# A mixture-of-experts block in fp32: expert blocks of 32 slots on four column groups instead of 64 on two, with the down product moved into the next block's gate-up

## The chip, the core and the metric

The kernel runs on one core of a Trainium2 chip. TensorE (PE) multiplies, VectorE (DVE) and ScalarE (ACT) work on elements, GpSimd (POOL) makes constants and some loads, and SyncE (SP) issues nearly all loads of weights. The metric is device time of one execution in microseconds. The kernel before takes 1511.01 us, the median of 3 runs from 1509.67 to 1511.81.

## The reference

One layer of a model of width 1024 on 256 tokens: a modulated norm, sparse attention and gated linear attention side by side, their merge, and a mixture of 32 experts, in fp32. The change touches the experts alone:

```python
logits = (xt @ router_w + router_b)            # xt 256 x 1024, 32 experts
top_v, top_e = lax.top_k(logits, TOP_K)        # TOP_K = 4
wts = jax.nn.softmax(top_v, axis=-1)
...                                            # tokens sorted by expert, padded to blocks
def expert_block(args):
    xb, e = args
    hgu = xb @ w_gate_up[e] + b_gate_up[e]     # w_gate_up[e] 1024 x 2048
    gate, up = jnp.split(hgu, 2, axis=-1)
    gate = jnp.minimum(gate, 7.0)
    up = jnp.clip(up, -7.0, 7.0)
    act = (up + 1.0) * (gate * jax.nn.sigmoid(1.702 * gate))
    return act @ w_down[e] + b_down[e]         # w_down[e] 1024 x 1024
out = segment_sum(ys * pw, ptok)               # weighted sum over each token's 4 experts
x = x + gt2 * out
```

The 256 x 4 assignments spread unevenly over the experts. All 32 experts get tokens, so all their weights, 32 x 12 MiB, are read once.

## The kernel before, in words

Everything up to the router (about 460 us) is written out in order and isn't touched. Its tables are made on VectorE: `table_n` holds the number of blocks, `table_e` the expert of each block, `table_w` what the load semaphores must have reached for that expert, `table_used` the block from which an expert's slots may be overwritten. A block is 64 slots (`SLOTS`) of one expert; an expert has as many blocks as its tokens need. Each engine then runs a loop over blocks, with the counts in registers.

One block on PE is: `gate_up` (L1380), eight pieces of 128 rows of the weights, each against 64 gathered tokens (`xg`); the 64 columns stand twice side by side on the array, so two column groups (q = 0, 1) work on different halves of the output. Between the first piece and the second stand the bias (L1387) and the scatter of the block before (L1355). Then come the gather of the next block's tokens (L1339, a product of `h2` with the 0/1 matrix `sel`), transposes of the slot weights (L1395), of the gathered tokens (L1348) and of the hidden values (L1402), and the down product (L1409), four pieces of 256 rows. ScalarE copies between the steps (`gx`, `xg`, `actT`, `selwT`, `ysb`) and computes the sigmoid; VectorE limits and multiplies the hidden values (`gcl`, `ucl`, `act_t`), makes `sel` and `selw` for the next block and, in `add_rows`, multiplies the scattered rows by `gt2` and adds them into `xs`.

The weights have one set of slots: eight `gu_slot` of 1 MiB (2048 columns, so runs of 8 KB) and four `dn_slot` of 1 MiB (two rows of 1024 for each partition, runs of 4 KB). SyncE goes through experts 1 to 31 in order and, for each slot, waits until its last load has landed and until the last block of the expert before has used it (`gu_used`, `dn_used`), then issues the load. It waits in order: a slot that isn't free holds all behind it.

Of the kernel before, what the change touches and what calls it, by code (L numbers as in the profile page):

```python
# [24 lines left out]
SLOTS = 64  # L25
# [42 lines left out]
def hybrid_block(nc, x, c, w_ada, b_ada, norm1_g, w_in, w_gate_lr, b_gate, gla_norm_g, w_branch_a, w_branch_b, w_out,  # L68
# [10 lines left out]
    MAXB = E + T * TOP_K // SLOTS  # L79
    NP2 = 4  # L80
# [16 lines left out]
    with ExitStack() as ctx:  # L97
# [11 lines left out]
        gu_slot = [sb(f"gu_slot{j}", 8 * j, [P, 2048]) for j in range(8)]  # L109
# [66 lines left out]
        def small(name, shape, dt=F32):  # L176
# [42 lines left out]
        le = sb("le", 187.5, [MAXB + 1, E])  # L219
        eofc = sb("eofc", 187.75, [MAXB + 1, 1])  # L220
        eofw = sb("eofw", 177, [MAXB + 1, 3 * E])
# [3 lines left out]
        eof = small("eof", [1, MAXB + 1])  # L225
        need_w = small("need_w", [1, MAXB + 1])
        table_e = small("table_e", [1, MAXB + 1], I32)
        table_w = small("table_w", [1, MAXB + 1], I32)
# [4 lines left out]
        of_block = small("of_block", [3 * E, MAXB + 1])  # L233
# [6 lines left out]
        xg = sb("xg", 128, [P, 4, P])  # L240
        gx = sb("gx", 130, [P, 512])
        gcl = sb("gcl", 132, [P, 512])
        sig = sb("sig", 134, [P, 512])
        ucl = sb("ucl", 136, [P, 512])
        act_t = sb("act_t", 138, [P, 512])
        actT = sb("actT", 140, [P, 4, P])
        ysb = sb("ysb", 142, [P, 512])
        sel = sb("sel", 144, [P, TT, SLOTS])
        selw = sb("selw", 144.5, [P, TT, 2, SLOTS])
# [4 lines left out]
        junk2 = sb("junk2", 132, [P, D])  # L254
# [3 lines left out]
        sum_bank = [[bank[6], bank[7]], [bank[4], bank[5]]]  # L258
# [23 lines left out]
        gu_in = [sem(f"gu_in{j}") for j in range(8)]  # L282
        dn_in = [sem(f"dn_in{j}") for j in range(4)]
        bgu_in, bd_in = sem("bgu_in"), sem("bd_in")
        gu_used = [sem(f"gu_used{j}") for j in range(8)]
        dn_used = [sem(f"dn_used{j}") for j in range(3)]
        bias3_ready = sem("bias3_ready")
        row_scaled, row_added = [sem(f"row_scaled{q}") for q in range(2)], sem("row_added")
# [5 lines left out]
        actT_full, actT_out, y_full, y_out, sc_full, acc_out = (  # L294
            sem(n) for n in ("actT_full", "actT_out", "y_full", "y_out", "sc_full", "acc_out"))
# [5 lines left out]
        def tile(name):  # L301
            return bank[NUMBER[name] % 8]
# [28 lines left out]
        def _(sp):  # L331
            def load_expert_piece(e, j):

                if j < 8:
                    sp.dma_start(gu_slot[j][:], w_gate_up[0, e, j * P:(j + 1) * P, :] if isinstance(e, int) else  # L335
                                 w_gate_up[0, ds(e, 1), j * P:(j + 1) * P, :].rearrange("a p n -> p (a n)")).then_inc(gu_in[j], 16)
                else:
                    i = j - 8
                    rows = slice(2 * i * P, 2 * (i + 1) * P)
                    sp.dma_start(dn_slot[i][:], w_down[0, e, rows, :].rearrange("(i p) n -> p i n", p=P) if isinstance(e, int) else  # L340
                                 w_down[0, ds(e, 1), rows, :].rearrange("a (i p) n -> p (a i) n", p=P)).then_inc(dn_in[i], 16)

            for n, (kind, i, last) in enumerate(PIECES):
                if n >= NP2:
                    wait_tile(sp, PIECES[n - NP2][2])
                sp.dma_start(piece[n % NP2][:], piece_source(kind, i)).then_inc(piece_in[n % NP2], 16)
                if kind in ("wa", "wb"):
                    wait_tile(sp, "o3")
                    load_expert_piece(0, 8 + 2 * (kind == "wb") + i)
            for j in range(8):  # L350
                user = [last for n, (_, _, last) in enumerate(PIECES) if n % NP2 == j // 2][-1]
                wait_tile(sp, user)
                load_expert_piece(0, j)
# [15 lines left out]
        def _(pool):  # L369
# [34 lines left out]
            for i in range(3):  # L404
# [6 lines left out]
                                allow_small_or_imprecise_dtypes=True))  # L411
            for i in range(3):
# [7 lines left out]
        def _(act):  # L420
# [200 lines left out]
            act.wait_ge(gath_full, 1)  # L621
            step(A(gx[:], bank[2][:], ACT.Copy), gx_out)
            act.wait_ge(gxT_full, 1)
            step(A(xg[:].rearrange("p j s -> p (j s)"), bank[3][:], ACT.Copy), xg_out)
            act.wait_ge(tables_ready, 1)
            nb = act.value_load(table_n[0:1, 0:1], min_val=1, max_val=MAXB)
            with act.Fori(0, nb) as g:
                g1_ = act.snap(g + 1)
                g2_ = act.snap(g + 2)
                act.wait_ge(gcl_ready, g1_)  # L630
                A(sig[:], gcl[:], ACT.Sigmoid, scale=ALPHA).then_inc(sig_ready, 1)  # L631
                act.wait_ge(gath_full, g2_)
                A(gx[:], bank[2][:], ACT.Copy).then_inc(gx_out, 1)  # L633
                act.wait_ge(gxT_full, g2_)
                A(xg[:].rearrange("p j s -> p (j s)"), bank[3][:], ACT.Copy).then_inc(xg_out, 1)  # L635
                act.wait_ge(actT_full, g1_)
                A(actT[:].rearrange("p c s -> p (c s)"), bank[4][:], ACT.Copy).then_inc(actT_out, 1)  # L637
                act.wait_ge(selwT_full, g1_)
# [817 lines left out]
```

## Time and profile before

| | |
|---|---|
| median of 3 runs | 1511.01 us |
| span of the profiled execution | 1508.0 us |
| last matmul of the expert stage ends | 1496.8 us |
| expert stage starts (first gather) | 463.2 us |
| PE, weight loads, DVE, ACT busy | 92%, 41%, 30%, 17% of the span |
| mean granted clock of PE | 0.987 |
| DMA moved | 483.37 MB, mean 321 GB/s |
| of it expert weights | 384 loads of 1 MiB |

The profile holds one execution, of which the span is given; no time of its own beside the span is on the page, and the median of the runs is 3.0 us above that span. Shares are means over stages with different limits, so the rows further down are taken stage by stage. An fp32 product of PE shows as two instructions, which is why counts of matmul instructions are twice those in the code.

### The profile page before, as it was taken

To read this page: it belongs to the slowest core of one execution; us is meant where nothing else is said; L and a number is where in the kernel's file an instruction comes from. 1 tells how busy PE (TensorE), PEld (TensorE's weight loads), DVE (VectorE), ACT (ScalarE), POOL (GpSimd) and SP (SyncE) were. 2 spreads that over 40 slices of the span, in tenths; PEclk is the share of its full clock that TensorE was granted. 3 is DMA by queue.
4 is the path that set the end of the run, shared out by engine and by line. 5 is a ranking of instruction groups with operands and counts; after the bars stand their busy time and mean duration, and the time that the engine had idled before them with its cause. 6 is when DMAs were issued, how large, how long until landed. Compare 5 with 4: busy or idle time off the path is not lost.

```text
span 1508.0 us, 17239 instructions
## 1 busy us (share of the span) xinstructions
PE 1394.2 (92%) x6390; PEld 618.8 (41%) x6391; DVE 449.9 (30%) x965; ACT 253.3 (17%) x433; POOL 10.6 (1%) x34
## 2 busy tenths in 40 slices
PE   0999999999987999999999999999999999989996
PEld 0788545777742333333333333333333333323331
DVE  0160024112234333233233333332332332323233
ACT  1330014210011111111111111111111111111111
POOL 0000000000000000000000000000000000000000
PEclk9999999999987999999999999999999999999998
DMA  8734343587743584999699999979999999999995
GB/s 273 279 112 168 118 161 112 173 281 287 295 187 128 207 334 159 418 416 419 277 399 418 418 416 419 419 312 417 416 419 418 417 416 419 419 417 416 419 419 206
DMA packets 117687, 483.37 MB, mean 321 GB/s; under 512 B 14738, under 2 KB 14866, under 8 KB 84802
## 3 DMA queue, kind: packets, MB, share of 16 engines
q1 hardware_dynamic: 108368, 477.13, 79.4%
q0 software_dynamic: 1056, 4.06, 0.9%
q10 hardware_dynamic: 8242, 1.89, 0.6%
q8 instruction: 15, 0.25, 0.1%
q14 instruction: 6, 0.05, 0.0%
HBM read 482.00 MB, written 1.05 MB: 320 GB/s over the span
## 4 chain that ended last, share of the span: by engine, by line
PE 72%; DMA 10%; SPq 8%; ACT 4%; ACTq 2%; issue 1%; DVE 1%; DVEq 0%
PE bank L1380 23%; PE bank L1073 14%; PE bank L1409 13%; DMA gu_slot<-in_w_gate_up 10%; PE bank L1082 7%; SPq L335 4%; SPq L340 4%; PE bank L1339 4%; PE bank L1355 3%; PE bank L1061 2%; PE bank L1348 1%; ACT gx L633 1%; ACT xg L635 1%; ACT actT L637 1%; ACTq L428 1%
## 5 line engine op out<-in xcount | busy, mean ns | idle before, releaser
L1380 PE MATMUL bank<-gu_slot,xg 128*64 128x512 f32 x2304 | 518.2, 597 | 16.3 <-DMA gu_slot<-in_w_gate_up 15.4
L1380 PEld LDWEIGHTS bank<-gu_slot,xg 128*64 128x64 f32 x2304 | 159.2, 137 | 363.7 <-issue 310.5
L1409 PE MATMUL bank<-dn_slot,actT 128*64 128x512 f32 x1152 | 255.1, 595 | 24.7 <-ACT actT L637 24.7
L993 DVE TENSOR_TENSOR rowt<-bank,gt 128x512 f32<-128x512 f32 x144 | 92.7, 685 | 398.6 <-PE bank L1355 397.3
L1073 PE MATMUL bank<-hT,piece 128*128 128x256 f32 x704 | 153.7, 380 | 0.0
L1409 PEld LDWEIGHTS bank<-dn_slot,actT 128*64 128x64 f32 x1152 | 79.5, 137 | 177.2 <-issue 143.9
L1073 PEld LDWEIGHTS bank<-hT,piece 128*128 128x128 f32 x704 | 133.3, 190 | 19.9 <-issue 2.0
L631 ACT ACTIVATE sig<-gcl 128x512 f32<-128x512 f32 x36 | 22.7, 630 | 569.3 <-DVE gcl L1011 569.3
L1011 DVE TENSOR_SCALAR gcl<-bank 128x512 f32<-128x512 f32 x36 | 24.9, 691 | 272.1 <-PE bank L1380 272.1
L997 DVE TENSOR_TENSOR xs<-xs,rowt 128x512 f32<-128x512 f32 x144 | 93.1, 688 | 2.5
L1082 PE MATMUL bank<-piece,hT 128*128 128x512 f32 x192 | 83.4, 593 | 0.0
L1339 PE MATMUL bank<-h,sel 128*64 128x512 f32 x296 | 71.6, 605 | 3.0 <-DVE sel L965 3.0
L1355 PE MATMUL bank<-ysb,selwT 64*128 64x512 f32 x288 | 72.1, 619 | 0.0
L641 ACT ACTIVATE ysb<-bank 128x512 f32<-128x512 f32 x36 | 21.5, 597 | 248.9 <-PE bank L1409 248.9
L1061 PE MATMUL bank<-piece,silc 128*32 128x512 f32 x192 | 24.8, 642 | 34.1 <-DVE silc L674 34.1
L1082 PEld LDWEIGHTS bank<-piece,hT 128*128 128x128 f32 x192 | 36.2, 190 | 44.3 <-issue 44.2
L631 ACT ACT_TABLE_LOAD x36 | 46.2, 1283 | 0.9 <-issue 0.3
L1339 PEld LDWEIGHTS bank<-h,sel 128*64 128x64 f32 x296 | 21.5, 139 | 45.7 <-issue 45.7
L1355 PEld LDWEIGHTS bank<-ysb,selwT 64*128 64x128 f32 x288 | 25.0, 188 | 32.5 <-issue 32.5
L1348 PE MATMUL bank<-ident,gx 128*128 128x128 f32 x148 | 24.7, 290 | 12.5 <-ACT gx L633 11.8
L1073 PE MATMUL bank<-yaT,piece 128*128 128x256 f32 x128 | 28.0, 379 | 0.0
L1073 PE MATMUL bank<-ybT,piece 128*128 128x256 f32 x128 | 28.0, 379 | 0.0
(274 smaller groups left out, 771.6 us busy)
## 6 DMA issues: line engine op xcount, KB each, us to landing
gu_slot<-in_w_gate_up SPq DMA_DIRECT2D x256, 1024.0 KB, 17.2
dn_slot<-in_w_down SPq DMA_DIRECT2D x128, 1024.0 KB, 17.1
piece<-in_w_in SPq DMA_DIRECT2D x17, 2048.0 KB, 7.8
piece<-in_w_ada SPq DMA_DIRECT2D x12, 2048.0 KB, 15.0
piece<-in_w_branch_a SPq DMA_DIRECT2D x2, 2048.0 KB, 7.9
piece<-in_w_branch_b SPq DMA_DIRECT2D x2, 2048.0 KB, 8.6
piece<-in_w_out SPq DMA_DIRECT2D x2, 2048.0 KB, 10.3
xs<-in_x ACTq DMA_DIRECT2D x1, 1024.0 KB, 13.2
```

Of the source, the lines that this page charges most:

```text
L335: sp.dma_start(gu_slot[j][:], w_gate_up[0, e, j * P:(j + 1) * P, :] if isinstance(e, int) else w_gate_up[0, ds(e, 1), j * P:(j + 1) * P, : ...
L340: sp.dma_start(dn_slot[i][:], w_down[0, e, rows, :].rearrange("(i p) n -> p i n", p=P) if isinstance(e, int) else w_down[0, ds(e, 1), rows ...
L631: A(sig[:], gcl[:], ACT.Sigmoid, scale=ALPHA).then_inc(sig_ready, 1)
L993: ins = V.tensor_tensor(rowt[:, t, :], sum_bank[t][q][:], gt2[:, cols_], ALU.mult)
L997: ins = V.tensor_tensor(xs[:, t, cols_], xs[:, t, cols_], rowt[:, t, :], ALU.add)
L1061: ins = M(ps[32 * q:32 * q + 32, :], silc[:, k, :], w[:, k, :], start=(r == 0), stop=(r == 1), tile_position=(0, 32 * q))
L1073: ins = M(ps[:, f * T:(f + 1) * T], w[:, k, a:a + P], src[:, k, :], start=(k == 0), stop=(k == KT - 1))
L1082: ins = M(ps[:], src[:, k, t * P:(t + 1) * P], w[:, k, :], start=(k == 0), stop=(k == KT - 1))
L1339: ins = M(bank[2][64 * q:64 * q + 64, :], sel[:, t, :], h2[:, t, 512 * q:512 * q + 512], start=(t == 0), stop=(t == TT - 1))
L1355: ins = M(sum_bank[t][q][:], selwT[64 * q:64 * q + 64, t * P:(t + 1) * P], ysb[64 * q:64 * q + 64, :], start=True, stop=True)
L1380: ins = M(bank[u][64 * q:64 * q + 64, :], xg[:, k % 4, 64 * (k // 4):64 * (k // 4) + 64], gu_slot[k][:, cols_], start=(k == 0), stop=(k == ...
L1409: ins = M(bank[5][64 * q:64 * q + 64, :], actT[:, f % 4, 64 * (f // 4):64 * (f // 4) + 64], dn_slot[f // 2][:, f % 2, 512 * q:512 * q + 51 ...
```

## The change

Blocks have 32 slots (`SLOTS = 32`, `GROUPS = 4`). The 32 columns of a block stand on four column groups, each for a quarter of the outputs. Gate-up takes its weights in four pieces of 256 rows; a partition holds two neighbouring rows, so a `gu_slot` is 2 MiB in runs of 16 KB, and a `dn_slot` 1 MiB in runs of 8 KB. The transposes pick every second column to match (`(i r) -> r i`).

The loop is skewed: the down product of a block is done within the gate-up of the next, after its second piece and the next gather; its scatter follows the last gate-up piece. Block 0 is written out ahead of the loop, and the last down and scatter behind it. The four sum banks stay in PSUM through the whole loop: `bias_rows` starts them, each scatter adds (`start=False`), and VectorE reads them once at the end, so `add_rows` is gone. The copy of `actT` moves from ScalarE to VectorE. Elementwise steps have 256 columns instead of 512.

```diff
-SLOTS = 64
+SLOTS = 32
+GROUPS = 4
...
-        gu_slot = [sb(f"gu_slot{j}", 8 * j, [P, 2048]) for j in range(8)]
+        gu_slot = [sb(f"gu_slot{j}", 16 * j, [P, 2, 2, D]) for j in range(4)]
...
+        hid_bank, y_bank, turn_bank, xgT_bank = bank[4], bank[5], bank[6], bank[7]
+        sum_bank = [[bank[0], bank[1]], [bank[2], bank[3]]]
...
+            def load_gate_up(e, q):
+                rows = slice(2 * P * q, 2 * P * (q + 1))
+                sp.dma_start(gu_slot[q][:].rearrange("p r u n -> p (r u n)"),
+                             w_gate_up[0, e, rows, :].rearrange("(p r) n -> p (r n)", r=2) if isinstance(e, int) else
+                             w_gate_up[0, ds(e, 1), rows, :].rearrange("a (p r) n -> p (a r n)", r=2)).then_inc(gu_in[q], 16)
...
             with sp.Fori(1, E) as e:
                 free = sp.value_load(table_used[0:1, ds(e, 1)], min_val=1, max_val=MAXB + 1)
-                for j in range(12):
-                    here, used = (gu_in[j], gu_used[j]) if j < 8 else (dn_in[j - 8], (dn_used + [y_full])[j - 8])
-                    sp.wait_ge(here, 16 * e)
-                    sp.wait_ge(used, free)
-                    load_expert_piece(e, j)
+                for q in range(4):
+                    sp.wait_ge(gu_in[q], 16 * e)
+                    sp.wait_ge(gu_used[q] if q < 3 else gu_full, free)
+                    load_gate_up(e, q)
+                for q in range(4):
+                    sp.wait_ge(dn_in[q], 16 * e)
+                    sp.wait_ge(dn_used[q] if q < 3 else y_full, free)
+                    load_down(e, q)
...
+            def hidden(full_count, count):
+                dve.wait_ge(gu_full, full_count)
+                V.tensor_scalar(gcl[:], hid_bank[:, 0:256], LIMIT, None, ALU.min).then_inc(gcl_ready, 1)
+                V.tensor_scalar(ucl[:], hid_bank[:, 256:512], LIMIT, -LIMIT, ALU.min, ALU.max).then_inc(ucl_ready, 1)
+                dve.wait_ge(sig_ready, count)
+                V.tensor_tensor(gcl[:], gcl[:], sig[:], ALU.mult).then_inc(gs_ready, 1)
+                dve.wait_ge(gs_ready, count)
+                V.scalar_tensor_tensor(act_t[:], ucl[:], 1.0, gcl[:], ALU.add, ALU.mult).then_inc(act_ready, 1)
+                dve.wait_ge(actT_full, count)
+                V.tensor_copy(actT[:].rearrange("p r s -> p (r s)"), turn_bank[:, 0:256]).then_inc(actT_out, 1)
...
+            def gate_up(q, landed):
+                pe.wait_ge(gu_in[q], landed)
+                for r in range(2):
+                    for c in range(GROUPS):
+                        ins = M(hid_bank[32 * c:32 * c + 32, :], xg[:, r, 32 * q:32 * q + 32],
+                                gu_slot[q][:, r, :, 256 * c:256 * c + 256], start=(q == 0 and r == 0), stop=(q == 3 and r == 1))
+                ins.then_inc(gu_used[q] if q < 3 else gu_full, 1)
...
+            def down(landed):
+                for pair in range(2):
+                    for h in range(2):
+                        pe.wait_ge(dn_in[2 * pair + h], landed)
+                    for r in range(2):
+                        for half in range(2):
+                            for h in range(2):
+                                c = 2 * pair + h
+                                a = 32 * (2 * half + h)
+                                ins = M(y_bank[a:a + 32, :], actT[:, r, 32 * c:32 * c + 32],
+                                        dn_slot[c][:, r, 512 * half:512 * half + 512],
+                                        start=(pair == 0 and r == 0), stop=(pair == 1 and r == 1))
+                                if r == 1 and half == 1:
+                                    ins.then_inc(dn_used[c] if c < 3 else y_full, 1)
...
+            with pe.Fori(1, nb) as g:
...
+                pe.wait_ge(xg_out, g1_)
+                gate_up(0, landed)
+                gate_up(1, landed)
+                pe.wait_ge(actT_out, g)
+                pe.wait_ge(sel_ready, g2_)
+                gather()
+                pe.wait_ge(selw_out, g)
+                down(landed_before)
+                gate_up(2, landed)
                 pe.wait_ge(selw_ready, g1_)
+                gate_up_bias()
+                gate_up(3, landed)
+                pe.wait_ge(y_out, g)
+                scatter()
                 pe.wait_ge(gx_out, g2_)
                 gather_transposes()
+                weight_transposes()
                 pe.wait_ge(act_ready, g1_)
+                hidden_transposes()
```

How the instructions stand now and before, on PE, within one turn of the block loop (names: `gu_slot`, `dn_slot` weights, `xg` gathered tokens, `h_85` or `h_81` the tokens `h2`, `bias_66` or `bias_62` the biases; a row is one or more equal instructions, with the semaphores it waits for). Before:

```order
L1380 MATMUL bank<-gu_slot_60,xg 64x512 [waits gu_in7]
L1380 MATMUL bank<-gu_slot_60,xg 64x512 x3
L1391 REGISTER_ALU
L1339 MATMUL bank<-h_85,sel 64x512 [waits sel_ready]
L1339 MATMUL bank<-h_85,sel 64x512 x3
L1395 MATMUL bank<-ident,selw 128x128 [waits ucl_ready]
L1348 MATMUL bank<-ident,gx 128x128 [waits gx_out]
L1348 MATMUL bank<-ident,gx 128x128 x3
L1402 MATMUL bank<-ident,act_t 128x128 [waits act_ready,acc_out]
L1402 MATMUL bank<-ident,act_t 128x128 x3
L1409 MATMUL bank<-dn_slot_61,actT 64x512 [waits dn_in0,actT_out]
```

Now, from the top of the turn to behind the down product's start:

```order
L1398 MATMUL bank<-gu_slot_53,xg 32x512 [waits gu_in0,xg_out]
L1398 MATMUL bank<-gu_slot_53,xg 32x512 x7
L1398 MATMUL bank<-gu_slot_54,xg 32x512 [waits gu_in1]
L1398 MATMUL bank<-gu_slot_54,xg 32x512 x7
L1472 REGISTER_ALU [waits actT_out]
L1371 MATMUL bank<-h_81,sel 32x256 [waits sel_ready]
L1371 MATMUL bank<-h_81,sel 32x256 x7
L1417 MATMUL bank<-dn_slot_57,actT 32x512 [waits dn_in1,dn_in0,selw_out]
```

The gather and the down product have moved between the second and the third gate-up piece, and the down product there is that of the block before.

On SyncE, one expert's loads before:

```order
L335 ISA [waits gu_used6,gu_in6]
L335 DMA gu_slot_59<-in_w_gate_up 128x2048
L335 ISA [waits gu_used7,gu_in7]
L335 DMA gu_slot_60<-in_w_gate_up 128x2048
L340 ISA [waits dn_used0,dn_in0]
L340 DMA dn_slot_61<-in_w_down 128x2x1024
```

and now:

```order
L338 ISA [waits gu_used2,gu_in2]
L338 DMA gu_slot_55<-in_w_gate_up 128x4096
L338 ISA [waits gu_full,gu_in3]
L338 DMA gu_slot_56<-in_w_gate_up 128x4096
L344 ISA [waits dn_used0,dn_in0]
L344 DMA dn_slot_57<-in_w_down 128x2048
```

The order of the loads is the same; they are eight for an expert instead of twelve, and each waits for one piece of twice the rows in gate-up.

## Rows read from the trace of the kernel before

**Rows 1.** The page: busy us and share of PE, and GB/s in 40 slices

```profile
PE 1394.2 (92%) x6390; PEld 618.8 (41%) x6391; DVE 449.9 (30%) x965; ACT 253.3 (17%) x433; POOL 10.6 (1%) x34
GB/s 273 279 112 168 118 161 112 173 281 287 295 187 128 207 334 159 418 416 419 277 399 418 418 416 419 419 312 417 416 419 418 417 416 419 419 417 416 419 419 206
```

**Rows 2.** Chain that ended last, one block: start us, us, what

```profile
499.91 1.72 PE bank L1380 x8
501.63 0.44 PE bank L1387 x4
502.06 1.92 PE bank L1355 x8
503.98 12.17 PE bank L1380 x56
516.15 1.74 PE bank L1339 x8
...
518.56 0.67 PE bank L1348 x4
...
527.55 1.72 PE bank L1380 x8
```

**Rows 3.** The same chain late in the span, two experts apart

```profile
1391.90 25.29 DMA gu_slot<-in_w_gate_up
...
1452.17 25.26 DMA gu_slot<-in_w_gate_up
```

**Rows 4.** Windows: stretch us, busy us (instructions) by engine, granted clock, DMA share, GB/s

```profile
509.50:530.00 20.50, 19.48 (x96) 6.94 (x94) 3.96 (x10) 4.53 (x7) 0.00 (x0) 1.00 0.00 0
563.50:585.50 22.00, 20.98 (x104) 7.45 (x102) 5.02 (x12) 4.53 (x7) 0.00 (x0) 1.00 0.00 2
...
1040.00:1480.00 440.00, 410.29 (x1910) 136.99 (x1906) 137.33 (x271) 68.03 (x105) 0.00 (x0) 1.00 1.02 418
```

**Rows 5.** Timeline of SyncE's queue, gate-up loads of experts 1 and 2

```profile
473.28 16.63 SPq L335 DMA_DIRECT2D gu_slot<-in_w_gate_up  x8
...
529.51 15.67 SPq L335 DMA_DIRECT2D gu_slot<-in_w_gate_up  x8
```

**Rows 6.** Timeline of PE, four column groups in use at L1061

```profile
41.51 1.93 PE L1061 MATMUL bank<-piece,silc 128*32 128x512 f32 x16
43.37 2.84 PE L1099 MATMUL bank<-inv,modp 128*128 128x1 f32 x24
```

**Rows 7.** Timeline, one elementwise step of 512 columns

```profile
1419.21 0.69 DVE L1011 TENSOR_SCALAR gcl<-bank 128x512 f32<-128x512 f32 x1 [9.40 <-PE bank L1380]
```

**Rows 8.** Windows: gate-up pieces (first two), down pieces (last)

```profile
443.00:450.00 7.00, 4.16 (x24) 2.10 (x24) 2.98 (x7) 2.85 (x7) 0.00 (x0) 0.59 1.01 428
1400.00:1415.00 15.00, 13.90 (x65) 4.20 (x64) 5.16 (x8) 1.88 (x2) 0.00 (x0) 1.00 1.01 422
1418.00:1426.00 8.00, 6.98 (x36) 2.67 (x34) 3.96 (x10) 2.65 (x5) 0.00 (x0) 1.00 1.02 409
```

**Rows 9.** DMA issues in 462 to 478: KB, us to landing

```profile
gu_slot<-in_w_gate_up SPq DMA_DIRECT2D x1, 1024.0 KB, 4.8
```

**Rows 10.** Windows around the router and the first block

```profile
440.00:444.00 4.00, 0.15 (x2) 0.00 (x0) 2.55 (x10) 2.73 (x6) 0.00 (x0) 1.00 0.88 328
...
462.00:469.30 7.30, 4.79 (x12) 1.57 (x12) 2.69 (x23) 1.20 (x2) 0.00 (x0) 0.50 0.00 0
469.30:475.00 5.70, 5.66 (x16) 1.82 (x18) 0.00 (x0) 1.28 (x1) 0.00 (x0) 0.50 0.18 26
475.00:480.00 5.00, 5.00 (x26) 1.62 (x24) 3.54 (x6) 0.00 (x0) 0.00 (x0) 1.00 0.54 197
```

**Rows 11.** Chain ahead of the first block (its start at 469.34)

```profile
463.17 3.70 PE bank L1339 x8
...
469.34 3.68 PE bank L1380 x8
```

**Rows 12.** Chain at the end, VectorE's second half

```profile
1496.86 1.30 DVE rowt L1024 x2
```

More of the change, by code:

```diff
@@ L239, in hybrid_block @@
         rowt = sb("rowt", 176, [P, TT, 512])
[L240 to L247, printed above, removed]
+        gx = sb("gx", 128, [P, 256])
+        xg = sb("xg", 129, [P, 2, P])
+        gcl = sb("gcl", 130, [P, 256])
+        ucl = sb("ucl", 131, [P, 256])
+        sig = sb("sig", 132, [P, 256])
+        act_t = sb("act_t", 133, [P, 256])
+        actT = sb("actT", 134, [P, 2, P])
+        ysb = sb("ysb", 136, [P, 512])
         sel = sb("sel", 144, [P, TT, SLOTS])
-        selw = sb("selw", 144.5, [P, TT, 2, SLOTS])
+        selw = sb("selw", 144.5, [P, TT, GROUPS, SLOTS])
         selwT = sb("selwT", 145.5, [P, T])
@@ L1324, in _ @@
             pe.wait_ge(eofc_ready, 1)
[L1325 removed]
+            full(M(ps[0:3 * E, 0:NT], eofw[:], ident[0:NT, 0:NT], start=True, stop=True))
             ps = begin("wt")
@@ L1332, in _, with gather @@
             full(ins)
[L1335 removed]
+            def gather():
                 for t in range(TT):
[L1338 to L1339 removed]
+                    for c in range(GROUPS):
+                        ins = M(turn_bank[32 * c:32 * c + 32, 0:256], sel[:, t, :], h2[:, t, 256 * c:256 * c + 256],
                                 start=(t == 0), stop=(t == TT - 1))
[L1341 to L1342 removed]
@@ L1353, in scatter @@
+            def scatter(last=False):
                 for t in range(TT):
@@ L1366, in _ @@
             gather_transposes()
-            with pe.Fori(0, nb) as g:
+            pe.wait_ge(xg_out, 1)
+            pe.wait_ge(selw_ready, 1)
+            for q in range(3):
+                gate_up(q, landed0)
+            gate_up_bias()
+            gate_up(3, landed0)
+            pe.wait_ge(sel_ready, 2)
+            gather()
+            pe.wait_ge(bd_in, 16)
+            wait_out(pe, "wt")
+            bias_rows()
+            pe.wait_ge(gx_out, 2)
+            gather_transposes()
+            weight_transposes()
+            pe.wait_ge(act_ready, 1)
+            hidden_transposes()
+            with pe.Fori(1, nb) as g:
                 g1_ = pe.snap(g + 1)
@@ L1403, in _ @@
-                ins.then_inc(actT_full, 1)
-                pe.wait_ge(actT_out, g1_)
-                for f in range(KT):
-                    if f % 2 == 0:
-                        pe.wait_ge(dn_in[f // 2], landed)
-                    for q in range(2):
-                        ins = M(bank[5][64 * q:64 * q + 64, :], actT[:, f % 4, 64 * (f // 4):64 * (f // 4) + 64],
-                                dn_slot[f // 2][:, f % 2, 512 * q:512 * q + 512], start=(f == 0), stop=(f == KT - 1))
-                    if f % 2 == 1:
-                        ins.then_inc(dn_used[f // 2] if f < KT - 1 else y_full, 1)
@@ L1428, in _ @@
-            bias_rows(0)
-            pe.wait_ge(selw_out, pe.snap(nb + 1))
-            pe.wait_ge(y_out, pe.snap(nb + 1))
-            last_rows(0)
-            bias_rows(1)
-            last_rows(1)
+                hidden_transposes()
+            pe.wait_ge(actT_out, nb)
+            pe.wait_ge(selw_out, nb)
+            landed_last = pe.value_load(table_w[0:1, ds(nb - 1, 1)], min_val=16, max_val=16 * E)
+            down(landed_last)
+            pe.wait_ge(y_out, nb)
+            scatter(last=True)
```

253 lines of the change are left out of this document (119 added, 134 removed).

## The prediction, written before the result was known

> **What bounds the kernel now.** I read the page first. TensorE (PE) is busy 92% of the span and the DMA rate sits near 418 GB/s from the middle of the span on [rows 1], so two limits lie close together. The chain of waits through one expert block tells which one binds early: a block of 64 slots takes 27.63 us (499.91 to 527.55), all of it PE work but for a few copies [rows 2]. Each expert's weights are 12 MiB, 12.58 MB, and late in the span two experts lie 60.27 us apart in that chain (1391.90 to 1452.17), 30.13 us each [rows 3]. So single-block experts settle on the DMA rate, and PE waits for it little. The stretches show the other half: the DMA moved nothing in 509.5 to 530 and in 563.5 to 585.5, but 418 GB/s in 1040 to 1480 [rows 4]. SyncE's queue says why: it starts expert 1's gate-up loads at 473.28 and can start expert 2's only at 529.51, two blocks of 27.63 us and 1 us later [rows 5]. There is one set of weight slots. While an expert has a further block, its slots are in use and the next expert's load can't start.
>
> How many blocks each expert has is set by the input. The reference's router on its own input gives the 32 experts 2, 127, 71, 46, 36, 3, 24, 88, 50, 22, 16, 23, 33, 11, 17, 99, 61, 5, 28, 28, 7, 3, 9, 30, 27, 16, 15, 37, 2, 20, 16, 52 tokens. In blocks of 64 that is 36, with two blocks for experts 1, 2, 7 and 15. In blocks of 32 it is 49: four blocks for experts 1 and 15, three for 2 and 7, two for 3, 4, 8, 12, 16, 27 and 31, one for the rest.
>
> **A block after the change.** Gate-up stays at 64 matmul instructions of 512 columns, on four column groups. With two groups 56 took 12.17 us, 217 ns each [rows 2]. The trace has four groups in use at L1061: 16 in 1.86 us from start to start, 116 ns each with the drain of so short a run [rows 6]; I take half of 217, 109 ns: 7.0 us. Down is 32 of the same: 3.5. Bias: half of 0.44, 0.2. Gather: 16 instructions of 256 columns, a quarter of 1.74/8 each, 0.9. Scatter stays 1.9. Transposes: 6 for 10 at 0.67/4, 1.0. Sum 14.5 us. The loop turn now stands behind the last transposes, with two register loads ahead of the first gate-up and no long matmul run to hide them; unseen on PE, between 0 and 0.8 us, I take 0.5. Block: **15.0 us** (14.5 to 16). The activation chain costs nothing while it is covered: gcl, sig, product and act_t at 256 columns are some 0.4 us each (0.69 at 512 [rows 7]), 2.1 us in all, beside scatter and four transposes, 2.6 us; uncovered it would add up to 2 us. The four multiplies and four adds of expert rows into xs on VectorE go away (the sums stay in PSUM); they lay beside PE, whose wait for them has no row in the block's chain. PE's total falls from 36 x 27.6 = 995 us to 49 x 15.0 = 735, so PE is no longer the bound: the weights of experts 1 to 31, 390 MB, need 933 us at 418 GB/s. What decides is how fast they come and how often the queue stands still.
>
> **The transfers.** 8 KB packets came at 422 GB/s and 4 KB ones at 409 [rows 8]; 8.39/0.422 + 4.19/0.409 = 30.1 us, the cycle of [rows 3]. Over 16 engines that is 311 ns for 8 KB and 160 for 4 KB, so about 10 ns of each packet is not bytes. 16 KB would take 612 ns, 428 GB/s, and a cycle 19.6 + 9.9 = **29.5 us**. No trace here has 16 KB packets. The bounds are 30.1 (longer runs give nothing) and 28.9 (no cost beside the bytes: 151 ns per 4 KB, 434 GB/s); I take the value the packet cost gives.
>
> **When the queue stands still.** Let L be when the last gate-up piece of an expert lands; its down pieces follow by L + 9.9. PE finishes that piece by L + 2.3, scatter, transposes and loop turn take 3.4, the next block's first gate-up piece 1.75: L + 7.5, and SyncE can issue at L + 7.9. A lone 1 MB load landed 4.8 us after its issue [rows 9]; 2 MB takes 2.5 more, 7.3. Unbroken the next piece would land at L + 14.8. An expert of two blocks thus loses 0.4 us, of three 0.4 + 15.0 = 15.4, of four 30.4. Experts 1 to 30: 6 x 0.4 + 2 x 15.4 + 2 x 30.4 = **94 us** of idle queue. Before it was 20.5 and 22 us behind experts 1 and 2 [rows 4], and the dips to 277 and 312 GB/s in [rows 1] are experts 7 and 15. The smaller blocks make the largest experts hold the slots longer while the stream needs them free.
>
> **The clock.** After 4 us with hardly a matmul (440 to 444) the granted clock is at half, 1.2 GHz; it is still there in 462 to 469.3, where PE works with gaps, and in 469.3 to 475, and back at full behind that, when PE has worked unbroken [rows 10]. In the new kernel PE is idle from about L + 6 to L + 14.8 in each single-block expert, so I expect its first gate-up piece at 1.2 GHz. The second piece lands at L - 9.9; behind it come the gather and the first half of down, which must free the first down slot by L - 2.35 (its next load would land at L + 2.45, 4.8 us after the issue). At full clock that is 1.75 + 0.9 + 1.75 + 0.4 us, L - 5.1, in time. At half clock all through it is 3.5 + 1.8 + 3.5 + 0.4, L - 0.7, 1.7 us late. From the second piece on PE works without a gap until past L, and in such a stretch the clock came back, so I take a value near the warm end, 0.35 us for each of the 26 experts among 1 to 30 with one or two blocks: **9 us** (0 to 44).
>
> The Trainium skill bears on this (TensorE: Matmul & The Clock Gate, Loop structure matters more than you think): a DMA wait ahead of each tile's matmuls makes every tile run cold. By that rule alone the term would be its upper end, 44 us; [rows 10] agree that a gap brings the half clock, and disagree that unbroken work stays cold.
>
> **Start and end.** Before the first block, at the half clock: gather 3.70 to 2.0 us, two copies and the transposes from there to 469.34 2.5 to 1.5 [rows 11], against 0.8 for two more register loads ahead of the first selection and the eight memsets that now stand first (an estimate, no row prices them there). So the block starts at 467.5 instead of 469.34. Its first gate-up piece (3.7 us, twice as many instructions as the eight of L1380 in [rows 11] at half the time each) is free at 471.2 instead of 473.28 [rows 5]; its 2 MB lands at 478.5, so the stream counts from 473.6. A late first down slot of expert 1 costs 1. End of the stream: 473.6 + 31 x 29.5 + 94 + 1 + 9 = 1492.1. Expert 31 has a second block, and its down is deferred: down 3.5, gate-up and bias 3.7, turn 3.0, actT 0.7, down 3.5, ysb 1.0, half the scatter 1.0, VectorE's first half twice 1.3, and from the start of its second half to the end 1508.0 - 1496.86 = 11.1 as now [rows 12]. That is 30.0: span 1522. The profiled execution has a span of 1508.0 and the median is 1511.0; with the same 3.0 us around it the time is **1525 us**, 14 more than before.
>
> **Rivals.** *Faster transfers.* With no cost beside the bytes a cycle is 28.9, 19 us less in all, and 1506. It needs the packet cost to be per packet and nothing else at 422 GB/s; that 8 KB packets gave 428 while PE was busy 4.16 us of 7 [rows 8] speaks for it, that they gave only 422 beside a busy PE against it. It decides the sign at a cycle of 28.95 us, or at 29.25 if the clock term is nil too. This is the case on the other side, 0.24 with its neighbours. The Trainium skill (DMA: Bandwidth & Descriptors, Where 436 GB/s comes from) gives 435 GB/s as the ceiling of the ports; an estimate from it is the same 28.9 us per expert. No row here shows more than 428 over a few us.
>
> *Cold clock.* If the clock stays at half until past L, every single-block cycle is 1.7 us longer and the time 1560: 0.12. For it: PE works only half of each cycle. Against it: nine us without a gap lie ahead of L.
>
> *Four groups give less than twice two.* At 20 us a block, each block that the queue waits out costs 5 us more (6 of them), and the way to the first release 1.2 us at ten experts: with the end some 45 us, 1570: 0.05. L1061 speaks against it.
>
> *Even.* Cycle 29.3 and no clock term, 1508 to 1514: 0.12.
>
> *The change does less than it says.* If 16 KB packets are no better (30.1), 31 x 0.6 adds 19: 1544, inside the forecast's side, 0.12.
>
> The forecast itself holds 0.35, between 1514 and 1538. A measurement of this kernel can't tell less than about 0.2%, 3 us, from no change. Faster (under 1508) 0.24, same 0.12, slower 0.64. The range for 8 in 10 runs from 1502, the fast transfers, to 1553, past the 16 KB case and short of the cold one.
>
> **What would show it.** In the changed profile: PE busy near 75% of the span and about half of a single-block stretch, DMA near full in most slices; four stretches without transfers, about 30, 15, 15 and 30 us long, behind experts 1, 2, 7 and 15; 29.5 us from one single-block expert to the next; some 16 gate-up instructions in 1.75 us; the granted clock falling to half once in each cycle; gate-up waiting for the DMA most. I am wrong if the cycle is under 29 us, if the clock holds the cycle over 31, or if the stretches without transfers sum to under 75 us.

## The result, and the profile after

The changed kernel takes **1539.4 us** (median of 4 runs, 1536.5 to 1548.5) against 1510.4 us for the kernel before on the same chip: ratio **1.0198** (95% interval 1.0180 to 1.0217), slower. The forecast was 1525 us (1502 to 1553), slower with 0.64. Sign and mechanism were right, the size was half of what came. The profiled execution has a span of 1534.7 us; the forecast span was 1522.

The page after (busy us and share by engine; GB/s in 40 slices; gate-up's matmuls with the idle time before them and its releaser; their DMA issues with KB and us to landing):

```profile
PE 1194.2 (78%) x8222; PEld 563.1 (37%) x8223; DVE 281.0 (18%) x852; ACT 191.7 (12%) x427; POOL 10.7 (1%) x35
GB/s 268 274 110 165 156 118 110 179 298 327 233 164 282 61 315 333 404 427 411 245 405 427 426 414 422 350 144 406 421 421 426 418 413 421 425 421 410 426 425 94
L1398 PE MATMUL bank<-gu_slot,xg 128*32 128x512 f32 x3136 | 428.3, 674 | 274.4 <-DMA gu_slot<-in_w_gate_up 241.7
gu_slot<-in_w_gate_up SPq DMA_DIRECT2D x128, 2048.0 KB, 15.8
```

PE fell from 92% of the span [rows 1] to 78%, though 49 blocks are computed instead of 36; gate-up now waits for transfers for 242 us. PE no longer bounds the whole: the dips in the GB/s row (61; 315 with 333; 245; 350 with 144) are the places where nothing comes.

Four stretches, a single-block stretch and a two-block expert, in windows (stretch, its length, busy us and instructions on PE, PEld, DVE, ACT, POOL, granted clock, DMA share, GB/s):

```profile
503.30:533.70 30.40, 28.03 (x256) 11.44 (x252) 6.51 (x22) 4.11 (x10) 0.00 (x0) 1.00 0.00 1
565.60:581.60 16.00, 14.84 (x138) 6.03 (x134) 3.25 (x11) 2.06 (x5) 0.00 (x0) 1.00 0.00 2
735.20:750.00 14.80, 13.64 (x129) 5.61 (x125) 3.25 (x11) 2.05 (x5) 0.00 (x0) 1.00 0.01 3
990.80:1021.80 31.00, 28.59 (x264) 11.71 (x260) 6.50 (x22) 4.11 (x10) 0.00 (x0) 1.00 0.00 1
1080.00:1340.00 260.00, 150.31 (x1102) 45.00 (x1105) 27.65 (x95) 17.27 (x43) 0.00 (x0) 0.76 1.00 421
612.00:643.00 31.00, 28.65 (x264) 11.72 (x260) 6.50 (x22) 4.11 (x10) 0.00 (x0) 1.00 0.97 403
```

The stretches without transfers behind experts 1, 2, 7 and 15 are 30.4, 16.0, 14.8 and 31.0 us: 92 us, where about 30, 15, 15 and 30 stood in the forecast. They answer to the 20.5 and 22 us of [rows 4]. These windows hold only the time in which nothing comes; their edges, where little comes, are not in the 92 us. In the single-block stretch PE works 58% of the time and the DMA all of it.

The chain of waits through one block inside a multi-block expert (start us, us, what), to be read beside [rows 2]:

```profile
547.64 3.64 PE bank L1398 x32
551.28 0.86 PE bank L1371 x16
552.14 3.43 PE bank L1417 x32
555.57 1.72 PE bank L1398 x16
557.29 0.22 PE bank L1404 x4
557.51 1.72 PE bank L1398 x16
559.23 1.92 PE bank L1427 x8
561.14 0.43 PE bank L1378 x2
561.58 0.22 PE bank L1384 x2
561.80 0.24 PE bank L1389 x2
562.04 1.20 issue
563.24 3.64 PE bank L1398 x32
```

Gate-up 7.1, gather 0.9, down 3.4, scatter 1.9, transposes 0.9, bias 0.2: 14.4 us of work. Behind it PE does nothing for 1.20 us that the profile can name: the loop turn with its register loads. The block is **15.60 us**.

When SyncE issues the first gate-up load of an expert (us), before and after, with two kernels that come below. An expert's interval, below, is the time to the first load of the next expert. Right behind an expert of several blocks it comes out short (23.9 us for expert 9), since SyncE then issues into an empty queue; so only sums over stretches that begin and end behind such experts can be compared to a few tenths:

| first load of expert | before | after | loop turned | before, long runs |
|---|---|---|---|---|
| 1 | 473.28 | 471.63 | 474.56 | 474.89 |
| 3 | 584.78 | 580.97 | 577.79 | 585.78 |
| 9 | 778.22 | 780.78 | 769.60 | 779.86 |
| 13 | 888.75 | 900.25 | 888.99 | 890.75 |
| 16 | 1001.12 | 1021.25 | 1008.13 | 1002.22 |
| 28 | 1350.78 | 1382.45 | 1363.47 | 1341.17 |
| 31 | 1440.25 | 1464.43 | 1445.85 | 1429.73 |
| end of span | 1508.0 | 1534.7 | 1515.3 | 1499.7 |

Rows of after of the kind from which that table and the intervals below come, experts 1, 4 and 5 (SyncE's queue; start us, us of issuing):

```profile
471.63 5.67 SPq L338 DMA_DIRECT2D gu_slot<-in_w_gate_up  x4
...
612.18 9.98 SPq L338 DMA_DIRECT2D gu_slot<-in_w_gate_up  x4
...
643.34 9.97 SPq L338 DMA_DIRECT2D gu_slot<-in_w_gate_up  x4
```

Up to expert 9 the rows of the two stay within 4 us of each other (the changed kernel 1.7 and 3.8 us ahead, then 2.6 behind). From 9 to 13 the kernel before goes at its PE's 27.6 us an expert, with weights that came in while an expert had two blocks; the changed one takes 29.9 us on average, near the transfers' time, and loses 9 us. From 13 to 16, over expert 15 with four blocks, it loses 8.6 more. The rest of the span adds 6.6.

### The profile page after: what moved, and what is told of

It is laid out like the page before. It is cut to its first block, busy times and chain, and to the rows that moved or that the text cites. A ratio compares the mean times of both kernels' runs of the same rounds, so it can differ in the third digit from the quotient of the medians.

```text
span 1534.7 us, 20943 instructions
## 1 busy us (share of the span) xinstructions
PE 1194.2 (78%) x8222; PEld 563.1 (37%) x8223; DVE 281.0 (18%) x852; ACT 191.7 (12%) x427; POOL 10.7 (1%) x35
## 3 DMA queue, kind: packets, MB, share of 16 engines
q10 hardware_dynamic: 8242, 1.89, 0.6%
## 4 chain that ended last, share of the span: by engine, by line
PE 63%; DMA 26%; issue 4%; SPq 3%; ACTq 2%; DVE 1%; ACT 1%; DVEq 0%
DMA gu_slot<-in_w_gate_up 26%; PE bank L1398 17%; PE bank L1105 14%; PE bank L1417 11%; PE bank L1114 7%; PE bank L1427 4%; PE bank L1371 3%; PE bank L1093 2%; SPq L344 1%; ACTq L438 1%; PE bank L1378 1%; SPq L338 1%; SPq L361 1%; PE bank L1306 1%; PE bank L1295 1%
## 5 line engine op out<-in xcount | busy, mean ns | idle before, releaser
L1398 PE MATMUL bank<-gu_slot,xg 128*32 128x512 f32 x3136 | 428.3, 674 | 274.4 <-DMA gu_slot<-in_w_gate_up 241.7
L1398 PEld LDWEIGHTS bank<-gu_slot,xg 128*32 128x32 f32 x3136 | 111.4, 118 | 519.2 <-issue 432.4
L1417 PE MATMUL bank<-dn_slot,actT 128*32 128x512 f32 x1568 | 177.8, 592 | 1.4 <-DVE actT L1017 1.4
L1010 DVE TENSOR_SCALAR gcl<-bank 128x256 f32<-128x256 f32 x49 | 20.8, 425 | 815.5 <-PE bank L1398 815.5
L1427 PE MATMUL bank<-ysb,selwT 64*128 64x512 f32 x392 | 97.4, 615 | 0.7 <-ACT ysb L649 0.7
L1417 PEld LDWEIGHTS bank<-dn_slot,actT 128*32 128x32 f32 x1568 | 55.8, 110 | 92.9 <-issue 86.1
L1371 PE MATMUL bank<-h,sel 128*32 128x256 f32 x800 | 57.4, 404 | 4.4 <-DVE sel L991 4.4
L1371 PEld LDWEIGHTS bank<-h,sel 128*32 128x32 f32 x800 | 31.1, 122 | 51.4 <-issue 45.5
L649 ACT ACTIVATE ysb<-bank 128x512 f32<-128x512 f32 x49 | 29.3, 597 | 152.5 <-PE bank L1417 152.5
L1017 DVE COPY actT<-bank 128x256 f32<-128x256 f32 x49 | 20.8, 425 | 49.7 <-PE bank L1389 49.7
L998 DVE TENSOR_SCALAR selw<-iota,slot_id,wts 128x128 f32<-128x128 f32 x100 | 29.6, 337 | 0.0
## 6 DMA issues: line engine op xcount, KB each, us to landing
xs<-in_x ACTq DMA_DIRECT2D x1, 1024.0 KB, 13.1
```

The costliest lines, as they stand in the source:

```text
L649: A(ysb[:], y_bank[:], ACT.Copy).then_inc(y_out, 1)
L998: ins = V.tensor_scalar(selw[:, t, :, :], iota[:].unsqueeze(1).to_broadcast([P, GROUPS, SLOTS]), slot_id[:, t, ds(e, 1)], wts[:, t, ds(e, ...
L1010: V.tensor_scalar(gcl[:], hid_bank[:, 0:256], LIMIT, None, ALU.min).then_inc(gcl_ready, 1)
L1017: V.tensor_copy(actT[:].rearrange("p r s -> p (r s)"), turn_bank[:, 0:256]).then_inc(actT_out, 1)
L1371: ins = M(turn_bank[32 * c:32 * c + 32, 0:256], sel[:, t, :], h2[:, t, 256 * c:256 * c + 256], start=(t == 0), stop=(t == TT - 1))
L1398: ins = M(hid_bank[32 * c:32 * c + 32, :], xg[:, r, 32 * q:32 * q + 32], gu_slot[q][:, r, :, 256 * c:256 * c + 256], start=(q == 0 and r = ...
```

## Experiments

**The changed kernel with short runs.** Loads and transposes as before the change, everything else as after.

```diff
-                sp.dma_start(gu_slot[q][:].rearrange("p r u n -> p (r u n)"),
-                             w_gate_up[0, e, rows, :].rearrange("(p r) n -> p (r n)", r=2) if isinstance(e, int) else
+                sp.dma_start(gu_slot[q][:].rearrange("p r u n -> p r (u n)"),
+                             w_gate_up[0, e, rows, :].rearrange("(r p) n -> p r n", r=2) if isinstance(e, int) else
...
-                    ins = nc.tensor.transpose(xgT_bank[:, r * P:(r + 1) * P], gx[:].rearrange("p (i r) -> p r i", r=2)[:, r, :],
+                    ins = nc.tensor.transpose(xgT_bank[:, r * P:(r + 1) * P], gx[:, r * P:(r + 1) * P],
```

> The changed kernel with runs of 8 KB (gate-up) and 4 KB (down) again, in the same eight loads for an expert. Theory (about 10 ns of each packet is not bytes): a single-block expert takes 0.6 us more, 30.4 us, at 21 of the 31 experts; those bound by PE's blocks don't change: +13 us, 1552. Rival (long runs or 2 MB pieces hurt the transfers, and that is why the time came out above the forecast): faster than the changed kernel, 1520 to 1536.

Measured 1560.8 us (1558.1 to 1564.6), ratio to the kernel before 1.0330 (1.0307 to 1.0354): 21 us slower than with long runs. In the single-block stretch (the same columns as above):

```profile
1080.00:1340.00 260.00, 154.77 (x1162) 46.47 (x1154) 29.26 (x99) 18.50 (x45) 0.00 (x0) 0.76 1.01 412
```

412 GB/s instead of 421. So the long runs pay, and by more than the 13 us expected from the packet cost; how much of it is packets is measured below.

**Both kernels with one block for each expert.** Tokens beyond the first block of an expert are left out, so 32 blocks in each.

```diff
             chain(V.tensor_reduce(blocks[:], over[:], AX.X, ALU.add))
+            chain(V.tensor_scalar(blocks[:], blocks[:], 1.0, None, ALU.min))
```

> The changed kernel with at most one block for each expert: 32 blocks instead of 49, tokens beyond the 32nd of an expert are left out. Theory (the loss is the queue standing still for experts of several blocks): no stretch without transfers, 30 cycles of 29.9 us from the first last-piece landing at 493 us, and 26 us behind the last: 1417 us, and the granted clock low in every cycle. Rival (clock or transfers themselves): cycles above 30.5 us, over 1435.

> The kernel before with at most one block for each expert: 32 blocks instead of 36, tokens beyond the 64th left out. Theory: transfers bind at 30.13 us an expert from the start, 934 us of stream from 476 and 17 to 20 us behind it: 1430 us, so that without further blocks the changed kernel is the faster by 10 to 15 us. Rival (the changed kernel is slower in itself): 1415 or less here.

Measured: 1420.85 us for the changed kernel, 1437.05 for the one before (one run each). From one expert to the next the changed kernel takes 29.70 us (499.84 to 1361.01, 29 cycles). The kernel before takes 29.80 over the same experts; its first ones go at PE's 27.6, and from expert 6 to 30 it is 30.12 (614.06 to 1336.96, 24 cycles). Windows of the changed one, then of the one before:

```profile
600.00:1000.00 400.00, 235.10 (x1746) 71.04 (x1750) 42.26 (x143) 27.09 (x66) 0.00 (x0) 0.77 1.00 424
```

```profile
600.00:1000.00 400.00, 368.81 (x1710) 122.00 (x1708) 122.39 (x245) 63.24 (x98) 0.00 (x0) 1.00 1.02 418
```

Without further blocks the change is 16 us faster; with them 29 slower. The cut takes 118.5 us from the changed kernel (17 blocks) and some 73 from the one before (4 blocks), so the loss lies in the experts with further blocks. The 14.8 us by which the spans differ (1419.1 against 1433.9) aren't all transfers: 8.7 lie between the first loads of experts 1 and 31, 9.7 behind the latter, and the changed kernel's run began its experts 3.6 us later (476.98 against 473.41).

**Short runs with one block for each expert.** The same cut, and the 8 and 4 KB runs.

> The changed kernel with every expert cut to one block of 32 slots (tokens beyond the 32nd of an expert are left out) and with weight runs of 8 and 4 KB in place of 16 and 8 KB. With long runs the same cut took 1420.85 us, 29.70 us from one expert to the next, and PE bounds no expert there. Theory, a packet costs about 10 ns beside its bytes: the cycle becomes 30.15 us, the time 1420.9 + 31 x 0.45 = 1435 us. Rival, the 21 us that short runs cost in the whole changed kernel are paid in every expert alike (0.68 us each): cycle 30.4, 1442 us. Rival, the long runs matter only where PE holds the slots: 1421 us.

Measured 1429.8 us, and 30.15 us a cycle (494.59 to 1368.82, 29 cycles), 0.45 more than with long runs, as the first theory has it. The agreement to the digit is luck: these are single runs, and such cycle times differ by up to 0.2 us between executions or variants without a known cause (29.85, 29.70 and 29.67 us in this document). The time is only 9 us more because in this execution the experts began 5.3 us earlier (471.70 against 476.98; the last section tells why); the first loads of experts 1 and 31 lie 897.1 us apart here, 884.0 there, 13.1 more. So the packet cost holds here, and in the whole kernel the short runs cost some 7 us beyond it. Three of the four two-block experts whose time can be read (3, 8, 16) stay at 31.2 us with either, expert 4 goes from 31.2 to 32.7. Of the 20.7 us between the first loads of experts 1 and 31, 9.1 lie between those of 9 and 16 (249.6 us against 240.5), though only five of these experts have a single block. Why isn't shown.

**The loop turned.** PE's loop is rotated so that its turn stands behind down, where PE has instructions queued; the work and its order are the same, but for one memset on VectorE ahead of the loop that makes `y_out` count from 1 (`this_half` is gate-up's third and fourth piece, bias, scatter and transposes).

```diff
-            with pe.Fori(1, nb) as g:
+            def next_half(count, landed_next, landed):
...
+                gate_up(0, landed_next)
+                gate_up(1, landed_next)
...
+                down(landed)
...
+            next_half((1, 2, 3), landed1, landed0)
+            with pe.Fori(1, pe.snap(nb - 1)) as g:
...
+                this_half(g1_, g2_, landed)
+                next_half((g1_, g2_, g3_), landed_next, landed)
...
+            this_half(nb, pe.snap(nb + 1), landed_last)
```

> The changed kernel with its PE loop turned, so that the register loads at the loop's top stand beside the down product's 3.4 us of matmuls. Theory (what a further block costs is the block's own length, of which 1.20 us is PE idle at the turn): a block takes 14.4 us instead of 15.6, the stretches without transfers shrink from 30, 16, 15 and 31 us by 1 to 3 us each, two-block experts fall from 31.2 us to 29.9, in all some 20 us: 1519 us. Rival (the half clock between single-block experts is the loss): the turn lies beside the DMA there, so nothing over 3 us: 1536.

Measured **1513.6 us** (1509.7 to 1517.7, 10 runs), ratio to the kernel before 1.0013 (0.9997 to 1.0028): no slower any more, and 5 us better than the 1519 expected. Chain of waits through one block:

```profile
561.18 3.64 PE bank L1399 x32
564.82 0.86 PE bank L1372 x16
565.68 3.43 PE bank L1418 x32
569.12 1.72 PE bank L1399 x16
...
575.58 0.02 issue
```

14.42 us: the 1.20 us are gone, and at the turn's new place, behind down (565.68 + 3.43 = 569.11), no gap stands either. The rows left out are the same but for 0.02 us. Expert 2 goes from 46.8 to 43.7 us, experts 3, 8 and 16 from 31.2 to 29.3, expert 4 to 30.1, single-block experts from 29.85 to 29.67 (experts 18 to 27). From expert 1's first load to expert 31's it is 971.3 us instead of 992.8, 21.5 less. The medians differ by 26; this profiled execution began its experts 2.9 us later than the other.

**The loop turned, one block for each expert.**

> The changed kernel with its PE loop turned, so that the turn's register loads stand behind down, and with every expert cut to one block of 32 slots (tokens beyond the 32nd of an expert are left out). Without the turned loop this cut took 1420.85 us, 29.70 us a cycle. Theory, the loop turn costs only where a further block of the same expert holds the slots: the cycle stays 29.7, and the stream begins 3 us later as it did in the whole kernel, so 1421 to 1425 us. Rival, the turn delays the release of the first gate-up slot in every expert: 1.2 us less in each cycle down to the 29.3 us that the transfers need, 1409 us.

Measured 1417.7 us, 29.68 us a cycle (495.19 to 1355.79) against 29.70. It began its experts 4.7 us earlier than the one-block cut without the turned loop, which is more than the 3.1 us between the two times. So here the turn costs nothing where the transfers set the cycle. (In the whole kernel the single-block cycle fell by 0.18 us with it; whether by the turn isn't shown.)

**Loop turned, and down earlier.** Down right behind the first gate-up piece, then the gather and the second piece, so that the first down slot comes free 2.6 us earlier. Against the turned loop:

```diff
                 gate_up(0, landed_next)
-                gate_up(1, landed_next)
...
+                down(landed)
                 pe.wait_ge(sel_ready, count[2])
                 gather()
-                pe.wait_ge(selw_out, count[0])
-                down(landed)
+                gate_up(1, landed_next)
```

> The turned loop with down right behind the first gate-up piece, ahead of gather and second piece. Theory: the first down slot is then free some 9 us before its load is due even at half clock, so the transfers never stop in single-block experts: 29.4 us a cycle instead of 29.9, at 20 experts: 9 us less than the turned loop, 1510. Against it: the second gate-up slot is free 3.4 us later in a further block, up to 0.6 us at ten experts. Rival (the cycle is set by the transfers alone, the clock costs nothing): the same as the turned loop.

Measured 1538.6 us, ratio 1.0174 (1.0148 to 1.0200): 25 us slower than without the new order, where 1510 was expected. The single-block stretch did get what was expected, 29.41 us a cycle (1080.88 to 1345.55) and 426 GB/s:

```profile
1080.00:1340.00 260.00, 153.83 (x1126) 49.73 (x1118) 29.25 (x99) 16.76 (x44) 0.00 (x0) 0.80 1.01 426
```

But in the first further block of an expert, down belongs to the expert's first block and waits for its own weights, which SyncE loads last. The chain of waits there:

```profile
552.47 3.46 PE bank L1418 x31
...
556.83 14.96 DMA dn_slot<-in_w_down
...
571.92 1.92 PE bank L1418 x16
...
574.71 3.43 PE bank L1399 x32
```

The second gate-up piece (574.71) now stands behind that wait, and with it the release of the slots: two-block expert 4 takes 32.2 us (615.39 to 647.61) instead of 30.1, experts 3, 8 and 16 some 30.4 instead of 29.3, expert 2 46.8 instead of 43.7. What was won on the single-block experts was more than lost on the eleven others.

**Idle time filled, one block for each expert.** Ten matmuls of 512 columns whose result isn't used stand at the end of each turn, to keep the clock up.

```diff
+                pe.wait_ge(xg_out, g2_)
+                for _ in range(10):
+                    M(xgT_bank[:], ident[:], h2[:, 0, 0:512], start=True, stop=True)
```

> The changed kernel with one block for each expert, and ten matmuls of 128 x 512 into a bank nobody reads at the end of each turn, 8.5 us of PE's 9 us of idle time. Theory of the clock (the half clock makes the first down slot late by 0 to 1 us): clock at full nearly all the time and cycles of 29.4 instead of 29.7 us, 8 us in all: 1412 us against 1420.9. Rival (the clock costs nothing): 1420.9 within 2 us, or more where the extra matmuls run into the next block.

Measured 1425.5 us, 4.7 more than without them where 8 less were expected, and 29.80 us a cycle. The timeline of PE (start us, us; the idle time before and its releaser in brackets):

```profile
924.52 2.31 PE L1490 MATMUL bank<-h,ident 128*128 128x512 f32 x5
928.17 1.92 PE L1399 MATMUL bank<-gu_slot,xg 128*32 128x512 f32 x16 [1.34 <-DMA gu_slot<-in_w_gate_up]
932.97 3.13 PE L1399 MATMUL bank<-gu_slot,xg 128*32 128x512 f32 x16 [2.87 <-DMA gu_slot<-in_w_gate_up]
935.85 1.60 PE L1372 MATMUL bank<-h,sel 128*32 128x256 f32 x16
```

The mean clock rose from 0.84 to 0.955 and the first piece is warm, 1.92 us; the second, after 2.87 us of waiting, still takes 3.13, and it is the second that stands ahead of the release. In the stretch from 1080 to 1340 the second piece took over 3 us in seven of nine cycles. So the experiment failed to make that piece fast, and what the half clock costs isn't settled by it.

**The kernel before with long runs only.** Gate-up in four loads of 2 MiB, 16 KB for each partition, down in 8 KB, transposes that pick every second column. Blocks, loop and sums as before.

```diff
-        gu_slot = [sb(f"gu_slot{j}", 8 * j, [P, 2048]) for j in range(8)]
+        gu_slot = [sb(f"gu_slot{j}", 16 * j, [P, 2, 2048]) for j in range(4)]
...
```

> The kernel before with the new runs alone: gate-up in four loads of 2 MiB with runs of 16 KB, down in runs of 8 KB, transposes of every second column; blocks of 64 on two groups and everything else as before. Theory: PE's 36 blocks of 27.63 us bind first, 995 us from 469.3 and 44 us behind it, 1500 us of span if it never waited; the transfers at 29.5 us let it wait little at the end: 1502 us, 0.5% faster than before and the best of all. Rival (2 MB pieces free and land later, so PE waits more): 1510 or above.

Measured **1505.6 us** (1501.7 to 1510.4, 12 runs), ratio 0.9963 (0.9948 to 0.9978): the best kernel here, 0.4% faster than the one before and 8 us faster than the turned loop on the same chip. Its late single-block stretch, which answers to the last of [rows 4]:

```profile
1040.00:1480.00 440.00, 412.32 (x1931) 144.27 (x1928) 140.13 (x277) 70.72 (x110) 0.00 (x0) 1.00 1.00 422
```

Up to expert 24 an expert takes 27.72 us, PE's time; from 25 on 29.52 (1252.61 to 1429.73, six cycles). In the kernel before the change from 27.64 to 30.09 (1139.31 to 1440.25, ten cycles) comes for good at expert 21. That is 0.57 us a cycle for the longer runs alone, the cleanest measure of them here. Of the 31 x 0.6 us that the transfers gained, 12 show between the first loads of experts 1 and 31 (954.8 us against 967.0); the rest would have lain where PE is the bound.

## Why the prediction was right, and where it failed

*What bounds the kernel.* Right. PE at 78%, a little over the forecast 75, gate-up waiting most for DMA.

*The block's work.* Right to 0.1 us: 14.40 against 14.5. The instruction counts at half of 217 ns each hold: 16 in 1.72 to 1.82 us.

*The loop turn.* **This step failed**, a term of the sum that was sized too small: "two register loads ahead of the first gate-up and no long matmul run to hide them; unseen on PE, between 0 and 0.8 us, I take 0.5". It is 1.20, beyond an upper bound that no row stood behind, in a place that was named rightly. The turned loop shows it by itself: 1.20 gone from the block, 21.5 us from the experts' stretch. By that rate the 0.7 us too few make some 12.5 us (an estimate), the size of the whole miss of the span (12.6).

*What it does to the queue.* "An expert of two blocks thus loses 0.4 us". With 15.6 us a block, two blocks are 31.2, longer than the 29.5 that their weights take, so such an expert is bound by PE: it lost 1.7. This is how the turn reached the time. Priced with the clock term at 30.25, experts 3, 4, 8 and 16 measured 31.2 (1.0 more; with 12 and 27 six such experts, 6 us if those two cost the same). Experts 1 and 2 together took 109.3 us against 105.8 forecast, experts 5 to 7 106.2 against 104.6, experts 13 to 15 121.0 against 119.6. Together 12 us; the other stretches give 2 back, as the difference. The stream of weights ended at 1502.5, forecast 1492.1:

```profile
1502.00:1503.00 1.00, 1.00 (x14) 0.31 (x8) 0.00 (x0) 0.00 (x0) 0.00 (x0) 1.00 0.46 188
1503.00:1504.00 1.00, 1.00 (x24) 0.68 (x19) 0.00 (x0) 0.00 (x0) 0.00 (x0) 1.00 0.00 0
```

*Transfers.* Right. The packet cost of 10 ns predicted 30.1 us with short runs and 29.5 with long ones. The blocks of 64 gave 30.09 and 29.52, the changed kernel's one-block cuts 30.15 and 29.70, and with down earlier the single-block cycle was 29.41. The rival of faster transfers (28.9) has nothing for it: no long stretch of single-block experts averaged under 29.4. That the cost is one per packet is a reading that fits these figures; the runs varied the run length only.

*The clock.* Right in size, and the mechanism is supported but not isolated. Single-block experts took 29.85 us (1076.30 to 1344.99, nine cycles), as forecast, 29.5 + 0.35; to the hundredth this is luck, as the transfers need 29.41 and the one-block cut took 29.70. The timeline of one such cycle:

```profile
1270.44 3.64 PE L1398 MATMUL bank<-gu_slot,xg 128*32 128x512 f32 x16 [10.20 <-DMA gu_slot<-in_w_gate_up]
1275.25 3.64 PE L1398 MATMUL bank<-gu_slot,xg 128*32 128x512 f32 x16 [1.16 <-DMA gu_slot<-in_w_gate_up]
1278.66 1.63 PE L1371 MATMUL bank<-h,sel 128*32 128x256 f32 x16
1280.12 3.61 PE L1417 MATMUL bank<-dn_slot,actT 128*32 128x512 f32 x32
1283.55 1.89 PE L1398 MATMUL bank<-gu_slot,xg 128*32 128x512 f32 x16
```

The first two pieces take 3.64 us at 1.2 GHz; the gather takes 1.63 where it takes 0.86 in the chain at full clock, and down is near full speed with 3.61, as the forecast's choice near the warm end said. Putting down ahead of gather and second piece took the cycle from 29.67 to 29.41, so a late first down slot costs about 0.3 us a cycle. That the half clock makes it late shows only from cycle to cycle: 5.5 to 8.5 us behind the start of a second piece that took 3.6 us (1245.74), then behind one that took 1.92 (1184.97), the windows of the changed kernel are

```profile
1251.24:1254.24 3.00, 3.00 (x32) 0.84 (x28) 0.00 (x0) 0.52 (x1) 0.00 (x0) 1.00 0.73 221
1190.47:1193.47 3.00, 2.66 (x28) 0.64 (x20) 0.00 (x0) 0.60 (x1) 0.00 (x0) 1.00 0.95 399
```

These are two of twelve such cycles; the deepest dips (221, 311 and twice 363 GB/s) all stand behind a slow second piece, but three slow ones had none (410 and twice 437). By the rule of the Trainium skill (TensorE: Matmul & The Clock Gate, Loop structure matters more than you think) a cycle would be cold throughout; here it isn't: the third piece, 8 us behind the last wait, takes 1.89 us for 16 instructions, and the 44 us at that end of the term did not come.

*Start and end.* The first slot came free at 471.63, forecast 471.2. Behind the end of the stream it is 32.2 us instead of 30.0. The same loop turn once more (1.23 us, ahead of expert 31's second block) puts the down of its first block at 1504.16, 1.7 us behind the end of the stream, where the forecast had it right there; and 0.9 stands between the copy of `actT` and the last down:

```profile
1498.43 1.23 issue
...
1514.09 0.44 DVE actT L1017
1514.53 0.89 issue
1515.42 3.70 PE bank L1417 x32
```

So 0.4 + 10.0 + 2.2 are the 12.6 us between 1522.1 and 1534.7. From 1534.7 to the median it is 4.7 us instead of the 3.0 assumed: the profiled execution was the fastest of the four.

*What wasn't weighed.* The forecast asked what the changed kernel would do, not why the kernel before was close to the transfers' time and still partly hid them: with two-block experts it had a lead of weights in its slots, and lived on it for five experts at 27.6 us each behind expert 7 and again behind expert 15, before its cycle rose to the transfers' 30.1. That it was a lead that PE used up is read from these intervals, not tested. The changed kernel has no use for a lead; its PE waits in every single-block cycle.

## What to carry to other kernels

When an engine stops being the bound, look at the one spot where it still is: here the way from a piece's landing to the release of its slot, in the experts with several blocks. A microsecond at a loop's turn is nothing where the loop waits for data and counts in full there; put the turn behind a long run of queued work. And split a change into its parts: the longer runs alone were worth more than the whole.

## What the runs showed of the hardware

- A loop turn on PE with its two table loads and their derived counts took 1.20 us with nothing queued to hide it, and left no gap behind a down product of 32 instructions (569.11 to 569.12 in the chain of the turned loop).
- 32 instructions of 512 columns on four column groups took 3.43 us, 107 ns each; on two groups 217 ns [rows 2]. The gain is the full factor of two.
- The same early code, untouched by any edit, came out some 5 us later in some executions, in which the granted clock fell. The windows of the changed kernel, then of its one-block cut, in which the expert stage began 5.3 us later:

```profile
48.00:52.00 4.00, 3.33 (x18) 2.78 (x19) 2.77 (x10) 1.88 (x5) 0.00 (x0) 1.00 1.04 385
```

```profile
48.00:52.00 4.00, 3.19 (x18) 0.68 (x10) 2.58 (x8) 0.60 (x1) 0.00 (x0) 0.50 1.05 387
```

In that cut the first product of `hT` with a `piece` (L1106) starts at 58.46, against 53.35 in the one-block cut with short runs, whose clock stayed up: 5.1 of the 5.3 us. The kernel before shows two groups of times as well (17 of 23 runs from 1507.3 to 1511.8 us, six from 1515.5 to 1516.0, at mean granted clocks of 0.986 to 0.990 and 0.983); where its clock fell isn't shown. A difference of 5 us between single runs of this kernel therefore says nothing until the start of the expert stage has been compared.
